# A hybrid model on one core: norms by token tile, broadcast rows made in the heads, a shorter router, each expert's weights loaded once

## The reference, cut to what matters

```python
logits = ht @ w_router + b_router
top_val, top_idx = lax.top_k(logits, TOP_K)           # TOP_K = 4 of 32
gates = softmax(top_val)
# per expert e, over its tokens in blocks of rows
hg = x @ w_gu[e] + b_gu[e]                            # 1024 -> 2048
glu, lin = minimum(hg[:, :1024], 7), clip(hg[:, 1024:], -7, 7)
y = (glu * sigmoid(1.702 * glu) * (lin + 1)) @ w_down[e] + b_down[e]
out[token] += gate * y
```

## Time and profile before

| | |
|---|---|
| median of 3 runs | 3281.84 us (3280.77 to 3284.49) |
| the profiled execution | 3280.83 us, its span on the engines 3279.0 us |
| TensorE matmul busy | 2777.9 us, 85% of the span |
| VectorE, ScalarE busy | 1363.4 us (42%), 546.8 us (17%) |
| moved from HBM | 1085.30 MB, 331 GB/s over the span |
| mean granted TensorE clock | 0.917 of full speed |

### The profile page before, as it was taken

One profiled execution on the slowest core, in us unless ns is written; L12 is line 12 of the kernel. 1 busy time (PEld: TensorE's weight loads), 2 busy tenths in 40 slices (PEclk: granted clock), 3 DMA queues, 4 the chain that ended last, 5 costly groups with the idle time before them and its releaser, 6 DMA issues.

```text
span 3279.0 us, 29868 instructions
## 1 busy us (share of the span) xinstructions
PE 2777.9 (85%) x10358; PEld 1415.3 (43%) x10358; DVE 1363.4 (42%) x3373; ACT 546.8 (17%) x1162; POOL 487.6 (15%) x521
## 2 busy tenths in 40 slices
PE   7898778777888997877777787559999999999997
PEld 6373333333355653333333374344444444444443
DVE  2447777776414367777775312451111111111112
ACT  1112222222104122222221102101111111111110
POOL 0014333333100033333333000000000000000000
PEclk9799998999988999889899887569999999999999
DMA  4669999999436299999999222047999999999996
GB/s 150 239 275 417 421 421 421 421 422 421 200 128 235 86 406 421 422 421 421 421 421 418 82 103 77 0 160 321 422 422 422 422 422 422 422 422 422 422 422 269
DMA packets 150565, 1087.45 MB, mean 332 GB/s; under 512 B 16752, under 2 KB 17008, under 8 KB 18864
## 3 DMA queue, kind: packets, MB, share of 16 engines
q1 hardware_dynamic: 75712, 546.34, 40.9%
q0 software_dynamic: 73904, 537.43, 39.5%
q10 hardware_dynamic: 864, 2.65, 0.2%
HBM read 1085.30 MB, written 1.05 MB: 331 GB/s over the span
## 4 chain that ended last, share of the span: by engine, by line
PE 58%; DMA 28%; DVE 8%; ACT 2%; issue 2%; DVEq 1%; SPq 1%; ACTq 0%
DMA big<-in_peer_uv,rows_of 18%; PE psum L777 12%; PE psum L504 11%; PE psum L413 9%; PE psum L804 6%; PE psum L425 6%; DMA uv_more<-in_peer_uv,rows_of 5%; DMA big<-in_moe 4%; PE psum L745 4%; PE psum L753 2%; DVE big L1226 2%; PE psum L771 2%; DMA ring<-in_ada 1%; PE psum L436 1%; SPq L384 1%
## 5 line engine op out<-in xcount | busy, mean ns | idle before, releaser
L504 PE MATMUL psum<-big,gdiag 128*128 128x512 f32 x1880 | 938.6, 657 | 257.2 <-ACT gdiag L878 257.0
L504 PEld LDWEIGHTS psum<-big,gdiag 128*128 128x128 f32 x1880 | 383.3, 210 | 809.4 <-issue 452.0
L1226 DVE CUSTOM_DVE_ANT_0 big<-psum,big 128x1024 f32<-128x1024 f32 x470 | 575.1, 1224 | 309.8 <-DMA big<-in_peer_uv,rows_of 304.7
L1608 POOL DMA_INDIRECT big<-in_peer_uv,rows_of x470 | 443.9, 945 | 1277.0 <-PE psum L504 763.9
L1575 DVE TENSOR_SCALAR big<-psum 128x512 f32<-128x512 f32 x35 | 24.2, 692 | 729.3 <-PE psum L777 729.3
L413 PE MATMUL psum<-big,ring 128*128 128x256 f32 x1280 | 283.9, 384 | 8.2 <-DVE big L1055 3.4
L413 PEld LDWEIGHTS psum<-big,ring 128*128 128x128 f32 x1280 | 245.9, 193 | 45.8 <-DVE big L1055 3.8
L804 PE MATMUL psum<-big 128*64 128x512 f32 x1120 | 248.1, 594 | 13.7 <-ACT big L1001 13.7
L777 PE MATMUL psum<-big 128*64 128x512 f32 x1120 | 249.7, 593 | 3.7 <-DMA big<-in_moe 3.7
L777 PE MATMUL psum<-ring,big 128*64 128x512 f32 x1120 | 247.3, 592 | 0.0
L425 PE MATMUL psum<-ring,big 128*128 128x512 f32 x480 | 212.8, 604 | 2.4 <-DVE big L1046 2.4
(11 more groups left out here) (333 smaller groups left out, 1968.8 us busy)
## 6 DMA issues: line engine op xcount, KB each, us to landing
big<-in_moe SPq DMA_DIRECT2D x280, 1024.0 KB, 20.2
ring<-in_moe SPq DMA_DIRECT2D x140, 1024.0 KB, 18.9
ring<-in_ada SPq DMA_DIRECT2D x24, 1024.0 KB, 7.4
ring<-in_peer_wq SPq DMA_DIRECT2D x16, 1024.0 KB, 7.3
ring<-in_mix_in SPq DMA_DIRECT2D x14, 1024.0 KB, 6.2
ring<-in_a_in SPq DMA_DIRECT2D x8, 1024.0 KB, 7.6
ring<-in_ple_gate SPq DMA_DIRECT2D x8, 1024.0 KB, 8.5
ring<-in_kv SPq DMA_DIRECT2D x8, 1024.0 KB, 6.4
```

Source lines behind the costliest of these rows:

```text
L504: mm = pe.matmul(psum[:, OUT_BANK[t] + c, :], gdiag[:, n % DIAGS, :], uv[(PICKS * l + n) % ROWS][:, D + c * 512:D + (c + 1) * 512], start= ...
L1226: j = dve.tensor_tensor_reduce(out=u, in0=x, in1=u, scale=1.0, scalar=0.0, op0=ALU.mult, op1=ALU.add, accum_out=dots[:, n:n + 1])
L1608: pool.indirect_dma_start(uv[g % ROWS], None, table, bass.IndirectOffsetOnAxis(rows_of[:, n:n + 1], 0)).then_inc(uv_loaded[g % ROWS], 16)
```

## The change

- `turn`, `gains`, `scales` and `scaled` work by token tile: tile 0 is squared, rooted, scaled and transposed before tile 1, and in `a_out`, `bo`, the peer parts and `ple` tile 0's norm stands ahead of tile 1's last addition. A shift is applied in the same pass as the gain. At the start the norm of x stands ahead of the softplus of lambda, and x comes in two loads.
- `spread` has no diagonals: the column is the stationary operand, broadcast, and the identity is streamed; ScalarE copies the row. final_norm's row is made at the beginning of the second `ple`, the four others in the dilated heads, one half per head.
- After mix_out ScalarE squares the tiles, VectorE multiplies them by the row, the gains and shifts of the experts' input are applied by ScalarE in its copy, and the rows of the untransposed input are applied later.
- The router takes the four largest by `max`, marks them with `match_replace`, and takes exponentials of all logits.
- Expert 0's first eight halves are issued when the recurrent heads end, the others when mix_out's slots are done. SyncE's loop is over the 32 experts and waits for the last block of the expert before. GpSimd runs over the blocks and passes each landed half on to TensorE (`w_here`).
- In a block the gather streams 512 columns with the one-hot as the stationary operand and is transposed afterwards (`turn_rows`), and the biases use four row tiles of 32 partitions. After the loop the sums are squared on ScalarE out of PSUM and stored by token tile.

```diff
 @block.sync
-            sp.wait_ge(cell_ready, 1)
-            n = sp.value_load(blocks[0:1, 0:1], min_val=E2, max_val=BLOCKS - 1)
-            with sp.Fori(0, n - 1) as i:
-                sp.wait_ge(cell_ready, i + 1)
...
+            sp.wait_ge(lasts_ready, 1)
+            for e in range(1, E2):
+                last = sp.value_load(lasts[0:1, e:e + 1], min_val=0, max_val=BLOCKS - 2)
                 for r in range(HALVES):
-                    sp.wait_ge(w_free, i * HALVES + (r + 1))
+                    sp.wait_ge(w_free, last * HALVES + (r + 1))
                     sp.dma_start(wring[r], w[e, r]).then_inc(w_loaded[r], 16)
 @block.gpsimd
+            with pool.Fori(0, n - 1) as i:
+                pool.wait_ge(cell_ready, i + 1)
+                pool.sem_inc(cell_seen, 1)
+                e = pool.value_load(cell[0:1, 0:1], min_val=0, max_val=E2 - 1)
+                pool.drain().then_inc(cell_taken, 1)
+                for r in range(HALVES):
+                    pool.wait_ge(w_loaded[r], e * 16 + 16)
+                    pool.sem_inc(w_here, 1)
 @block.tensor
+            def spread(n, vec, half):
+                if n:
+                    pe.wait_ge(row_taken, n)
+                for k in range(4):
+                    mm = pe.matmul(psum[:, 3, k * P:(k + 1) * P],
+                                   vec[:, 4 * half + k:4 * half + k + 1].to_broadcast([P, P]), ident,
+                                   start=True, stop=True)
+                mm.then_inc(row_done, 1)
...
                 mm.then_inc(da_turned, 1)
+                spread(2 + a, (rm, gf, shift_f, rf)[a // 2], a % 2)
                 pe.wait_ge(da_copied, a + 1)
...
+            def gather():
+                for t in range(TT):
+                    for c in range(2):
+                        mm = pe.matmul(psum[CAP * c:CAP * (c + 1), 2, :], S[:, t, :], hs[:, t, c * 512:(c + 1) * 512],
+                                       start=(t == 0), stop=(t == TT - 1), skip_group_check=True)
+                mm.then_inc(gather_done, 1)
+            def turn_rows(i):
+                pe.wait_ge(xg_taken, i)
+                for b in range(4):
+                    mm = pe.transpose(psum[:, 3, b * P:(b + 1) * P], xg[:, b * P:(b + 1) * P], ident)
+                mm.then_inc(xg_turned, 1)
...
-                        pe.matmul(psum[CAP * c:CAP * (c + 1), b, :], E, bgu[:, (2 * b + c) * 512:(2 * b + c + 1) * 512],
+                        r = slice(E2 * (2 * b + c), E2 * (2 * b + c + 1))
+                        pe.matmul(psum[CAP * c:CAP * (c + 1), b, :], E[r, :], bgu[r, :],
                                   start=True, stop=False, skip_group_check=True)
                 for k in range(KC):
-                    pe.wait_ge(w_loaded[k], i * 16 + 16)
+                    pe.wait_ge(w_here, i * HALVES + (k + 1))
...
-                pe.wait_ge(x_taken, i + 2)
+                turn_rows(i + 2)
 @block.scalar
             def ple(l, i):
                 act.wait_ge(v_done, PICKS * (l + 1))
                 act.dma_start(pT, d["pT"][l]).then_inc(p_loaded, 16)
                 act.dma_start(late, d["late"]).then_inc(late_loaded, 16)
-                root(i)
+                if l:
+                    for half in range(2):
+                        take_row(half, row_f, half)
+                roots(i)
...
+            for n in range(16, 20):
+                if n % 2 == 0:
+                    g = 2 + n // 2 - 8
+                    act.activation(hs[:, g % 2, (g // 2) * 512:(g // 2 + 1) * 512], tile_in(m + g), ACT.Square,
+                                   accum_out=ss4[:, g:g + 1]).then_inc(out_square, 1)
+                t = n // 2 - 8
+                root(n, t)
+                if n % 2:
+                    for b in range(2):
+                        act.wait_ge(turned, 32 + 2 * t + b + 1)
+                        for k in range(4 * b, 4 * b + 4):
+                            j = act.activation(xT[:, k, t * P:(t + 1) * P],
+                                               psum[:, 4 + 2 * t + b, (k % 4) * P:(k % 4 + 1) * P], ACT.Identity,
+                                               scale=gf[:, k:k + 1], bias=shift_f[:, k:k + 1])
+                        j.then_inc(xT_ready, 1)
 @block.vector
+            def normed(i, t):
+                square(t, h[:, t, :])
+                inverse(2 * i + t, t)
+                scaled(t)
...
+            for t in range(TT):
+                dve.match_replace(out=kept[:, t, :], in_to_replace=tk4[:, t, :], in_values=logit[:, t, :], imm_value=NEG)
+            dve.drain()
+            dve.tensor_scalar(member, kept, NEG, None, ALU.is_equal)
...
+            for t in range(TT):
+                dve.wait_ge(acc_square, t + 1)
+                variance(t)
+                dve.tensor_tensor(ysb[:, t, :], flat[t], row_o, ALU.mult)
+                inverse(20 + t, t)
+                dve.scalar_tensor_tensor(hs[:, t, :], ysb[:, t, :], rstd[:, t:t + 1], h[:, t, :], ALU.mult,
+                                         ALU.add).then_inc(y_ready, 1)
```

More of the change, by code:

```diff
@@ L531, in ple @@
             def ple(l, i):
+                if l:
+                    for half in range(2):
+                        spread(half, V8("final_norm"), half)
                 turn(i)
@@ L754, in scatter @@
                                        start=False, stop=stop, skip_group_check=True)
[L755 to L762 removed]
+                    if stop:
+                        mm.then_inc(moe_done, 1)
             n = pe.value_load(blocks[0:1, 0:1], min_val=E2, max_val=BLOCKS - 1)
@@ L808, in _ @@
             pe.wait_ge(out_taken, n + 1)
-            scatter(True).then_inc(moe_done, 1)
-            spread(4)
+            scatter(True)
         @block.scalar
@@ L912, in _ @@
             ple(0, 2)
-            root(3)
+            roots(3)
             m = tile0("kv")
@@ L942, in _ @@
             ple(1, 5)
-            root(6)
-            root(7)
+            for n in range(12, 16):
+                root(n, n // 2 - 6)
             m = tile0("mix_in")
@@ L1057, in _ @@
+            dve.memset(xb[:, :, 0:3], 0.0).then_inc(pads_ready, 1)
+            for t in range(TT):
+                dve.wait_ge(x_loaded, 16 * TT)
+                square(t, h[:, t, :])
+            for t in range(TT):
+                inverse(t, t)
+                scaled(t)
             dve.wait_ge(small_loaded, 32)
+            gains(0, V8("norm_mix0"))
             nl, t0, e1, s1, s2, pl = (tiny[:, i, :] for i in (2, 0, 1, 3, 4, 5))
@@ L1464, in _ @@
-            add_row_scaled(ysb, h)
-            scales(9, h)
-            scaled()
-            gains(8, gf, shift=shift_f)
-            spread(2, gf)
-            spread(3, shift_f, row2)
+                t, c = g % 2, slice((g // 2) * 512, (g // 2 + 1) * 512)
+                x = tile_in(m + g)
+                dve.wait_ge(out_square, g + 1)
+                dve.tensor_tensor(ysb[:, t, c], x, row_m[:, c], ALU.mult).then_inc(dve_took, 1)
+                if g >= 2:
+                    dve.drain()
+                    dve.tensor_tensor(ss[:, t:t + 1], ss4[:, t:t + 1], ss4[:, 2 + t:3 + t], ALU.add)
+                    dve.drain()
+                    variance(t)
+                    inverse(16 + 2 * t, t)
+                    dve.scalar_tensor_tensor(h[:, t, :], ysb[:, t, :], rstd[:, t:t + 1], h[:, t, :], ALU.mult, ALU.add)
+                    dve.drain()
+                    square(t, h[:, t, :])
+                    inverse(17 + 2 * t, t)
+                    scaled(t, ysb)
@@ L1476, in _ @@
             dve.drain()
+            for g in range(4):
+                dve.memset(E[E2 * g:E2 * g + 1, :], 1.0)
+            dve.tensor_copy(ident4[0:E2], ident[0:E2, 0:E2].unsqueeze(1).to_broadcast([E2, 4, E2]))
+            dve.drain().then_inc(E_ready, 1)
             dve.wait_ge(logits_done, 1)
```

487 lines of the change are left out of this document (238 added, 249 removed).

## The result

The changed kernel takes **3170.6 us** (median of 4 runs, 3168.8 to 3172.7); the kernel before, timed beside it, 3283.2. The ratio is 0.9656, with its 95% interval 0.964 to 0.9673. The forecast was 3166 in a range of 3143 to 3198. The profiled execution took 3172.7 and its span is 3170.8: 108.2 less than the span of 3279.0 before, where the prediction's terms add up to -115.

The account below looks back on a forecast made before the run. In the expert loop a block costs 29.2 us on TensorE and 29.9 on the DMA queues; before it, chains run one engine at a time. Terms sum to -115: 3280.8 - 115 = 3166 us, range 3143 to 3198.

Parts of the forecast that it names:

- The loop's mechanism: Expert loop: 21 blocks at TensorE's 27.2 us, 14 at the queue's 29.9, 32 sets loaded not 35; -41 us.
- less some 5 where the lead ends: Expert loop: deduction from the 14 queue-paced blocks where TensorE's lead over the loads runs out; 4 us in the sum.
- the norms around the rows and kv: Norms by tile around the experts' rows and kv: ple0 -2.2, ple1 +0.8, kv -2.0; -3.4 us in all.
- The heads: Dilated heads: a half spread of 1.75 us enters each of 8 heads' dependent chain, +1.2 each; +9.5 us.
- rival B: The heads hide their spread and TensorE's block is at 26.6 us, kernel 3153 us; chance 0.15.
- mix_out to the loop: Two terms: mix_out to logits -27.6 us (path 17.5), router to first gate matmul -16.5 us (17.9 plus 1.5).
- The start: Kernel start: chain begins with x's norm, softplus beside a_in, first matmul at 14.6 not 23.49; -8.9 us.
- the norms after a_out and bo: Tile 0's norm runs under the last tile's matmul, leaving tile 1's; -3.7 us each, -7.4 in all.
- ple 1 to mix_in: Norms between ple 1 and mix_in: spread, copy and diagonals gone, tile 0's norms under proj; -9.8 us.
- A: Rival: the block does not shorten, loop 35 x 29.2 = 1021 us, kernel 3201 us; chance 0.12.
- C: Rival: GpSimd's relay slows the loop, at 2.8 us a half 1176 us and the kernel 3356; chance 0.03.
- D: Rival: loads aren't saved, loop 35 x 29.9 = 1046 us, kernel 3226 us; chance 0.02.

Follow-up runs that it names:

- square of four kernels: Changed kernel with the shorter block, the saved loads, both or neither undone; loop 1042.2 (both undone), 1042.5 (block undone), 1023.7 (loads undone), 989.5 us (neither).
- e_warm: Changed kernel plus 12, 20, 16 and 12 idle identity transposes in the norms ahead of peer_q0, ple 0, kv and peer_q1; 3170.0 us, ratio 0.9649.
- e_best: Changed kernel with tile 0's root first in both ple, heads' spreads behind the products, 16 idle transposes ahead of ple 0; 3163.9 us, ratio 0.9619.
- e_best_swap: e_best with experts 1 and 9 also exchanged in storage (weights, biases, router columns); 3148.3 us, ratio 0.9574 to the kernel before.
- e_root: Changed kernel with ScalarE's root for tile 0 in both ple put ahead of its wait for all rows and its loads; 3164.7 us, ratio 0.9633.
- e_heads: Changed kernel with each head's spread moved behind the head's products and ScalarE's row copy one head later; 3172.7 us, ratio 0.9649.
- e_relay2: Changed kernel with GpSimd's relay of each landed half made of two counts and two waits, not one; 3173.2 us, ratio 0.9653.

## Why the prediction was right or wrong

**The loop's mechanism was right, point by point.** The block is 27.24 for 27.2, with each part as told (gather 1.87 for 1.9; bias 1.02 and 0.15 more in the gate's matmuls, where 1.15 stood for both; gap 1.46 for 1.45); the three stretches of TensorE's blocks are 0 to 8, 20 to 26 and 30 to 34, and 14 blocks are the queue's. 21 x 27.24 = 572 leaves 418, 29.86 a block. What failed is the last deduction, "less some 5 where the lead ends" (4 in the sum): the first waiting blocks (9 and 27) are only 0.8 shorter between them than the 29.84 of the queue, three others (14, 19, 29) take 30.55, some 2 more in all, and 990 came in place of 986. The square of four kernels shows the argument behind it: three sets less are worth 34 us, not 90, and only with a block faster than the queue. By the Trainium skill, "DMA: Bandwidth & Descriptors" (Specifications), about 358 GB/s is a core's share of HBM; the changed kernel's page, with this core running alone, has slices at 422, so here it did not bind.

**The terms that failed are the norms around the rows and kv: +6.5 where -3.4 stood.** Two things were missing. First the clock: I took every stage to start as it did before. The changed kernel, first 5 us of peer_q0, ple 0 and peer_q1:

```profile
156.40:161.40 5.00, 5.00 (x16) 4.10 (x17) 0.00 (x0) 0.00 (x0) 0.00 (x0) 0.66 0.13 54
874.00:879.00 5.00, 4.97 (x6) 2.19 (x7) 0.00 (x0) 0.00 (x0) 0.00 (x0) 0.50 0.00 0
...
1105.90:1110.90 5.00, 5.00 (x17) 4.20 (x18) 0.00 (x0) 0.00 (x0) 0.00 (x0) 0.71 0.15 59
```

and the kernel before, peer_q0 and ple 0:

```profile
169.30:174.30 5.00, 4.99 (x23) 4.42 (x24) 0.00 (x0) 0.00 (x0) 0.00 (x0) 1.00 0.00 0
883.10:888.10 5.00, 4.95 (x12) 2.32 (x13) 0.00 (x0) 0.00 (x0) 0.00 (x0) 1.00 0.00 0
```

A level of 0.50 is 1.2 GHz, and values between are a mixture of the two levels. With it the first group of ple 0 is 30.7 in place of 27.7, that of peer_q0 15.8 in place of 14.1 and that of peer_q1 15.5 in place of 14.1, 6.1 in all. No kernel that starts from the changed one has these three at their old length, but for ple 0 with idle transposes. What TensorE did ahead of them differs: before, 16 transposes in 3.6 us stood at the end of the norm, now eight of 1.98. e_warm shows that more transposes change it at ple 0 and don't at the others, so why each stage gets its level stays open. Nor is it the code alone: the group of ple 1 takes 29.4 in e_best and 27.7 in e_best_swap, which differ only in the order of the experts.

Second, ple 0's norm itself gained 1.5 (11.7 to 10.2) and not 2.2. That order of root, loads and additions was seen, but priced only as a rebate on the gain; e_root shows it is 3.3 and 5.8. The rest of +3.8 is the rows' stage (+1.9, inside what it varies by) and its last 16 matmuls at a lower clock (8.85 for 7.15). At ple 1 the norm itself is 12.8 for 11.7, +1.1 where +0.8 stood; the two clock terms are 1.4 and 1.7 there, and the rows' stage is 2.1 shorter. kv's norm gave 2.3 where 2.0 stood.

So of the 9.9 between +6.5 and -3.4 some 6.1 are the starts of the three stages, 3.4 the two last row groups, and about 0.7 the norms. The lower starts are in every kernel with the new norms, but for ple 0 with idle transposes. The last row groups are chance: kernels with the same code have 7.15 or 8.8 there. What failed is the step that took the old trace's clock for the new stages.

By the Trainium skill, "ScalarE: Activation LUTs" (What ACT_TABLE_LOAD costs), a switch is about 2.66 us, of which 1.28 are the table load and 1.38 a drain. The row of ple 0 has 1.28 for the load, as the earlier trace rows and as the page says, but the root starts 0.02 later: no drain shows, and the sum was right to go by the row.

**The heads: +5.8 for +9.5, right in sign and place.** The changed kernel, one head in the chain:

```profile
2002.25 0.90 PE psum L659 x3
2003.15 1.71 PE psum L457 x8
2004.86 0.32 PE psum L666 x2
```

The spread is 1.71 for the 0.58 of waiting, as told. Not told was that the first two products cost 0.32 behind it and not 0.69: a head lost 0.76 and not 1.2. Moving the spread (e_heads) won 0.55 a head and no time that could be measured; rival B's first half, that the heads hide it, fell.

**mix_out to the loop: -46.6 for -44.1.** From mix_out's last matmul to the copy of the logits are 19.9 for 17.5. ScalarE's 2.90 for eight scaled copies is in the chain, and the logits take 7.94 (both tiles with their biases) where 5.2 stood: the granted clock there is 0.50, and where the row of the forecast stood it was 0.87. From the copy on the 14.4 are less than 17.9 + 1.5: the tables' matmuls are 1.9 and not 3.7 (from 2164.10 to 2166.00), the down bias 1.07 and not 1.8, and the loop starts at the full clock (its first 5 us have 1.00), so that the 1.5 for a half clock was not to be paid.

**The rest.** The start is 0.4 off, the norms after a_out and bo 0.1; the end gained 1.6 more. ple 1 to mix_in lacks 2.1, 0.9 of it ple 1's group at a lower clock (30.7 for 29.7). The misses cancel in part: +10 around the rows and kv, +4 in the loop, +2 each at mix_in and before the logits, against -5 in the router, -4 in the heads and -3 at the end and in stages that were not in the forecast. That the time was met to 5 us owes something to that.

**The rivals.** A (a block of 29.2) fell: four row tiles run at once. B fell in its first half, and its block of 26.6 did not come. C and D fell to e_relay2 and to 384 loads in the page. Loading expert 0 early was worth nothing, as told.

## What to carry to other kernels

Where TensorE and the DMA queue are within a few per cent of each other, price a saving on one of them by running both through the blocks with the lead between them: what three loads less or 2 us a block less are worth depends on the other, and here the saved loads alone gave nothing, the shorter block alone a third of what both gave together. Put what an engine issues for others (a root, a scaling) ahead of its own wait and loads. When a norm between two stages changes, do not take the next stage's clock from the old trace: at three stages here it cost 1.4 to 3 us each, and at ple 0 that was more than the norm ahead had won.

## What the hardware showed that was not expected

- Four matmul row tiles of 32 partitions, each on its own output, take 1.02 for 8 instructions of 512 columns at the full clock, where one row tile takes 1.86.
- The first two products of a head take 0.32 behind the spread and 0.69 behind a wait. That their weights are loaded during the spread is the likely reason: the trace has that load starting at 2004.44, 0.42 before the spread ends, and in the kernel before only at the end of the wait, at 2045.30. No run separates it.
- A relay of DMA completions through GpSimd is free, and a second hop through the same engine too (989.2 for 989.5).
- Idle transposes ahead of a stage raised its clock at one place of four, but there in each of three kernels (27.7 for the first group, 29.2 to 30.8 without them).
